# Attention scores from split operands: the low half of the keys multiplied on 64 partitions instead of 128, and the two PSUM banks of a row on opposite halves

## Chip, core and metric

The kernel runs on one core of one Trainium2 chip. What is measured is device time in microseconds of one execution of the whole program. A core has the engines TensorE (PE in the profile, its weight loads PEld), VectorE (DVE), ScalarE (ACT), GpSimd (POOL) and SyncE (SP), which work side by side and wait for each other through semaphores.

## What is computed

Two layers of a decoder trunk on 1024 tokens of width 1024. Of each layer, the attention part is what matters here:

```
z = rms_norm(x) @ w_in                       # q | k | v | u, 512 columns each
q, k normed and rotated per head             # 8 heads of 64
s = q @ k.T                                  # per head, 1024 x 1024, causal dilated masks
p = exp(s - max); att = (p @ v) / sum(p)
x = x + concat(att, pool) @ w_out
x = x + hier_moe(rms_norm(x))                # 16 experts, top 2 in one of 4 groups
```

The three dilated windows of the reference are one causal mask with logarithms of counts, which is added to the scores, so that each head needs one score matrix.

## The kernel before

Everything is written out by hand, engine by engine, in one loop over the two layers. A layer has four stages: the input projection (`in_pe`), attention (from `scores` to the last `probs_v`), the output projection with the router (`out_pe`), and the expert blocks (`moe_pe`).

**How scores are made.** TensorE takes operands of type fp32r, which hold fewer bits than fp32. So q and k are each split in a high part and a low rest, and a score is the sum of three products: high q with high k, low q with high k, high q with low k. A head has 64 channels and TensorE sums over up to 128 partitions. For head `a` of a pair (0 or 1), `own` are the 64 partitions where its q and k lie, `other` the 64 partitions of the other head. The tile `q_parts[a]` holds high q on `own` and low q on `other`; `k_high[a]` holds high k on `own` and a copy of k on `other`; `k_low[a]` holds low k on `own` and zeros on `other`. Two products then make one bank of scores: `q_parts` with `k_high` over 128 partitions gives two of the three terms (L1763), `q_parts` with `k_low` over 128 partitions gives the third (L1765), in which the 64 rows of `other` only add zeros. The zeros are written by two memsets on VectorE in each layer (L1165, L1262).

**Rows.** A row `m` (64 in a layer, `ROWS_A`) is one head's tile of 128 queries, number `i = m % 8`, against all keys up to its own: (i + 1) x 128, in steps of 256. So tiles 0 and 1 have one product pair of 256 columns, tiles 2 and 3 one of 512, tiles 4 and 5 one of 512 and one of 256 in a second PSUM bank, tiles 6 and 7 two of 512 in two banks. In a layer that makes 96 products of each of the two kinds, and 192 in the program.

**The order around them.** On TensorE the loop for row m has: `scores(m + 2)`, then `probs_t(m)` (turns of 128 x 128 of the probabilities, L1657), then `probs_v(m - 1)` (probabilities with v, 128 x 64, L1789), at some places `mix` (pooling, L1806) and `att_t`. VectorE adds the mask and takes the maximum (`mask`, L1278), evacuates half of the turned probabilities (L1288), and prepares the next head: `q_low` (L1254) and `k_lower` (L1243). ScalarE takes the exponential (`exp`, L899), evacuates the other half (L917), and prepares the next head: `q_top` (L838), `k_top` (L842) and `k_other` (L846), at places 8 to 10 and 0 to 2 of 16 rows. The semaphore `staged` tells TensorE that a head's low parts are there, `k_copied` that the copy of k is.

Of the kernel before, what the change touches and what calls it, by code (L numbers as in the profile page):

```python
# [33 lines left out]
P = 128  # L34
DEPTH, SEQ, D = 2, 1024, 1024
HEADS, HD = 8, 64
# [77 lines left out]
def trunk(nc, x, norm1_gain, w_in, q_norm_gain, k_norm_gain, w_pool, pool_scale, w_out,  # L114
# [7 lines left out]
    with ctx:  # L122
# [100 lines left out]
        k_low = [part("k_low0", AT_A + 5120, SEQ), part("k_low1", AT_H1 + 2 * SEQ, SEQ)]  # L223
        att = kT_r.rearrange("p (a t c) -> p a t c", a=PAIRS, c=P)
# [58 lines left out]
        k_copied = sem("k_copied")  # L283
        s_done = sem("s_done")
# [490 lines left out]
        def _(a_):  # L775
# [5 lines left out]
            for s in (params, k_copied, q_high_in, k_high_in, win_top, gain_in, sd1, sqz_done, sdz, cat_top, v_copied, u_copied, pool_top, t_evac, p_ready, pt0_ev, at_ev, sd2,  # L781
                      ge_exp, dm_exp, silu_done, aT_ready, y1_ready, xg_half, xg_top, gu_top, may_clear):
                a_.sem_inc(s, BIAS)
# [34 lines left out]
            with a_.Fori(0, DEPTH) as l:  # L818
# [28 lines left out]

                def in_act(t, par_, h):
# [43 lines left out]
                evac_turned(1, T - 1, 2)  # L892

# [15 lines left out]
                for m in range(ROWS_A):  # L909
# [17 lines left out]
                    if n == 2:  # L927
                        k_other(p, 1)
                    if p < PAIRS - 1:
                        if n == 10:  # L930
                            k_other(p + 1, 0)
                        if n == 8:
                            a_.wait_ge(s_done, upto(l, ROWS_A, p * 16 + 8))
                            q_top(p + 1, 0)
                        if n == 9:
                            k_top(p + 1, 0)
                    elif n == 10:
                        a_.wait_ge(poolT_ready, upto(l, 2 * NG, 2 * NG))
                        sc.activation(pool_hi, poolT[:, :, 0:P], ACT.Copy).then_inc(pool_top, 1)
# [165 lines left out]
        def _(dve):  # L1105
# [54 lines left out]
            def first_q_low(l):  # L1160
                dve.wait_ge(q_high_in, upto(l, 2 * PAIRS, 1))
                ve.tensor_tensor(out=q_parts[0][HD:P, :], in0=qT[0:HD, 0, :],
                                 in1=q_parts[0][0:HD, :].bitcast(f32), op=ALU.subtract)
                dve.wait_ge(z_done, upto(l, 4 * T, 4 * T - 2))
                ve.memset(k_low[0][HD:P, :].bitcast(f32), 0.0)  # L1165
# [66 lines left out]
            with dve.Fori(0, DEPTH) as l:  # L1232
# [6 lines left out]
                def k_lower(p, a, n, c=slice(0, SEQ)):  # L1239

                    own = slice(HD * a, HD * (a + 1))
                    dve.wait_ge(k_high_in, upto(l, 2 * PAIRS + 1, n))
                    return ve.tensor_tensor(out=k_low[a][own, c], in0=kT[own, p, c],  # L1243
                                            in1=k_high[a][own, c].bitcast(f32), op=ALU.subtract)
# [16 lines left out]
                dve.wait_ge(tqk_done, upto(l, 3 * T, 3 * T))  # L1261
                ve.memset(k_low[1][0:HD, :].bitcast(f32), 0.0)  # L1262
# [384 lines left out]
        def _(pe):  # L1647
# [29 lines left out]
            with pe.Fori(0, DEPTH) as l:  # L1677
# [74 lines left out]
                def scores(m):  # L1752
# [5 lines left out]
                    if m >= 2:  # L1758
                        pe.wait_ge(sm_ready, upto(l, ROWS_A, m - 1))
                    nk = (i + 1) * P  # L1760
                    for c in range(0, nk, 512):
                        w = min(512, -(-(nk - c) // 256) * 256)
                        te.matmul(ps[:, 2 * b + c // 512, 0:w], q_parts[a][:, i * P:(i + 1) * P],  # L1763
                                  k_high[a][:, c:c + w], start=True, stop=False)
                        ins = te.matmul(ps[:, 2 * b + c // 512, 0:w], q_parts[a][:, i * P:(i + 1) * P],  # L1765
                                        k_low[a][:, c:c + w], start=False, stop=True)
# [307 lines left out]
```

## Time and profile before

| | us |
|---|---|
| median of 3 runs | 1547.82 (1545.84 to 1548.75) |
| the profiled execution, its own time | 1546.53 |
| its span in the trace | 1544.7 |
| TensorE busy | 1408.9 (91%) |
| VectorE busy | 959.9 (62%) |
| ScalarE busy | 679.8 (44%) |
| GpSimd busy | 363.2 (24%) |

The span runs from the first to the last instruction. Busy is time in which an engine had an instruction of the program in work; TensorE's ends are modelled and overlap, so what a product costs is read from the distance between two starts. Within the span the attention stage of the first layer lies at 216 to 371 us and that of the second at 969 to 1123 us.

### The profile page before, as it was taken

Reading aid. Unit: us, or ns where it says so; the run is one execution under the profiler, and the core shown is the slowest. Engines: PE = TensorE matmul, PEld = TensorE weight load, DVE = VectorE, ACT = ScalarE, POOL = GpSimd, SP = SyncE. Lnnn points to the kernel's source line nnn. Section 1 sums busy time; section 2 is a strip of 40 time slices with the busy share of each in tenths; the row PEclk is TensorE's granted clock in tenths of the full one; section 3 lists DMA queues with packets and bytes.
Section 4 is the critical chain, followed back from the end, with each engine's and each line's share of the span. In section 5 each row is a group of like instructions: output and inputs, shape, how many; then the busy total and the mean of one; then the engine's idle time right before and its main releaser. Section 6 shows DMA issues by size and latency. Waiting matters only on the chain.

```text
span 1544.7 us, 23882 instructions
## 1 busy us (share of the span) xinstructions
PE 1408.9 (91%) x7375; PEld 1121.7 (73%) x7376; DVE 959.9 (62%) x1955; ACT 679.8 (44%) x1044; POOL 363.2 (24%) x256
## 2 busy tenths in 40 slices
PE   7999999999996899999699999899999959999990
PEld 5887878888885666666478788788888846666660
DVE  6666576663567756666566656766546686666560
ACT  5232156764112554555522312776621145554550
POOL 1000039302000133332520000870110013322335
PEclk9999999999998899999899999999999979999995
DMA  8200020000126999995581001200002577999827
GB/s 301 71 0 1 1 110 1 1 1 15 55 83 248 293 343 339 341 289 120 98 222 73 1 1 34 77 1 1 15 28 82 197 249 211 335 284 335 267 43 136
DMA packets 115892, 204.74 MB, mean 133 GB/s; under 512 B 9816, under 2 KB 76576, under 8 KB 115776
## 3 DMA queue, kind: packets, MB, share of 16 engines
q1 hardware_dynamic: 90976, 130.78, 24.4%
q0 software_dynamic: 19136, 53.67, 15.5%
q10 hardware_dynamic: 5664, 18.88, 3.1%
q8 instruction: 57, 0.93, 0.3%
q14 instruction: 59, 0.48, 0.1%
HBM read 169.74 MB, written 49.28 MB: 142 GB/s over the span
## 4 chain that ended last, share of the span: by engine, by line
PE 61%; DMA 16%; DVE 9%; issue 8%; ACT 4%; DVEq 1%; POOL 1%; ACTq 0%; POOLq 0%
PE ps L1687 19%; DMA out_x<-x_res,arena 15%; PE ps L1835 10%; PE ps L1657 9%; PE ps L1789 7%; PE ps L1965 6%; PE ps L1981 4%; PE ps L1763 2%; PE ps L1869 2%; PE ps L1765 2%; DVE w_in_lo L1157 1%; PE ps L1806 1%; ACT x_res L1004 1%; DVE arena L1375 1%; DVE gu_lo L1522 1%
## 5 line engine op out<-in xcount | busy, mean ns | idle before, releaser
L1522 DVE TENSOR_TENSOR gu_lo<-big,gu_hi 128x2048 fp32r<-128x2048 f32 x96 | 217.7, 2290 | 161.1 <-ACT gu_hi L982 149.9
L743 POOL DMA_INDIRECT x_res<-token_rows,row_tok x62 | 105.4, 1700 | 419.4 <-PE ps L1657 154.6
L982 ACT ACTIVATE gu_hi<-big 128x2048 fp32r (+1 forms) x96 | 180.7, 1916 | 29.0 <-PE ps L1965 17.9
L1657 PEld LDWEIGHTS ps<-cst,arena 128*128 128x128 f32 x970 | 112.4, 141 | 78.5 <-DVE arena L1587 27.4
L1657 PE MATMUL ps<-cst,arena 128*128 128x128 f32 x970 | 144.4, 275 | 26.1 <-DVE arena L1587 9.6
L1981 PE MATMUL ps<-big,arena 128*128 x360 | 163.8, 598 | 4.6 <-issue 4.6
L755 POOL DMA_INDIRECT out_x<-x_res,arena x62 | 101.6, 1639 | 188.6 <-ACT x_res L1004 137.6
L1278 DVE CUSTOM_DVE_ANT_0 arena<-ps,cst 128x128 f32<-128x128 f32 (+7 forms) x128 | 95.4, 754 | 79.2 <-PE ps L1765 78.5
L1789 PE MATMUL ps<-big,arena 128*128 128x64 f32 x1152 | 142.5, 269 | 0.0
L1789 PEld LDWEIGHTS ps<-big,arena 128*128 128x128 f32 x1152 | 138.5, 192 | 0.7
L1687 PE MATMUL ps<-w_in_hi,hT_hi 128*128 128x512 f32 x512 | 132.9, 399 | 3.9 <-ACT w_in_hi L803 2.5
L1687 PE MATMUL ps<-w_in_lo,hT_hi 128*128 128x512 f32 x512 | 129.5, 393 | 2.3 <-DVE w_in_lo L1157 2.2
L1687 PE MATMUL ps<-w_in_hi,hT_lo 128*128 128x512 f32 x512 | 126.7, 389 | 0.0
L1981 PEld LDWEIGHTS ps<-big,arena 128*128 128x128 f32 x360 | 65.5, 192 | 70.7 <-issue 70.7
L1687 PEld LDWEIGHTS ps<-w_in_lo,hT_hi 128*128 128x128 f32 x512 | 96.1, 189 | 25.3 <-DVE w_in_lo L1157 5.3
L1687 PEld LDWEIGHTS ps<-w_in_hi,hT_hi 128*128 128x128 f32 x512 | 94.6, 190 | 22.6 <-ACT w_in_hi L803 2.6
L1687 PEld LDWEIGHTS ps<-w_in_hi,hT_lo 128*128 128x128 f32 x512 | 96.1, 188 | 20.0
L899 ACT ACTIVATE arena<-arena,st 128x128 f32<-128x128 f32 (+7 forms) x128 | 98.8, 772 | 26.9 <-DVE st L1278 26.1
L1965 PE MATMUL ps<-gu_hi,xgT_hi 128*128 128x512 f32 x360 | 103.6, 410 | 7.6 <-issue 7.0
L1004 ACT ACTIVATE x_res<-ps 128x512 f32<-128x512 f32 x45 | 26.9, 598 | 182.2 <-DMA out_x<-x_res,arena 145.2
L1657 PE MATMUL ps<-cst,x_res 128*128 128x128 f32 x616 | 83.6, 280 | 19.3 <-DMA x_res<-token_rows,row_tok 11.5
L1965 PE MATMUL ps<-gu_lo,xgT_hi 128*128 128x512 f32 x360 | 98.5, 396 | 0.0
(199 smaller groups left out, 2350.7 us busy)
## 6 DMA issues: line engine op xcount, KB each, us to landing
big<-in_w_gate SPq DMA_DIRECT2D x32, 1024.0 KB, 11.4
big<-in_w_up SPq DMA_DIRECT2D x32, 1024.0 KB, 15.8
big<-in_w_down SPq DMA_DIRECT2D x32, 1024.0 KB, 13.8
big<-in_w_in SPq DMA_DIRECT2D x14, 1024.0 KB, 9.2
big<-in_w_out SPq DMA_DIRECT2D x4, 2048.0 KB, 10.3
token_rows<-arena ACTq DMA_DIRECT2D x16, 512.0 KB, 2.7
out_x<-x_res ACTq DMA_DIRECT2D x16, 512.0 KB, 3.5
x_res<-out_x SPq DMA_DIRECT2D x8, 512.0 KB, 5.3
```

Source lines behind the costliest of these rows:

```text
L743: pool.indirect_dma_start(out=xg[slot], out_offset=None, in_=token_rows, in_offset=bass.IndirectOffsetOnAxis(ap=row_tok[:, j:j + 1], axis= ...
L755: pool.indirect_dma_start(out=out, out_offset=bass.IndirectOffsetOnAxis(ap=row_dst[:, j:j + 1], axis=0), in_=y[j % RING], in_offset=None, ...
L899: sc.activation(pr[m % 3][:, 0:nk], pr[m % 3][:, 0:nk], ACT.Exp, scale=-1.0, bias=st[:, 64 + m % 16:65 + m % 16], accum_out=st[:, 80 + m % ...
L982: sc.activation(gu_hi[(2 * slot + h) % 3], raw, ACT.Copy).then_inc(gu_top, 1)
L1278: ve.tensor_tensor_reduce(out=pr[m % 3][:, 0:nk], in0=ps[:, 2 * b:2 * b + 2, :].rearrange("p a c -> p (a c)")[:, 0:nk], in1=cst[:, C_MASK ...
L1522: ve.tensor_tensor(out=gu_lo[i], in0=raw, in1=gu_hi[i].bitcast(f32), op=ALU.subtract)\
L1657: ins = te.transpose(ps[:, bank + i // 4, (i % 4) * P:(i % 4 + 1) * P], src, ident)
L1687: ins = te.matmul(ps[:, 2 + 2 * par_ + i, :], a[:, k, :], b[:, k, :], start=opens and k == 0, stop=closes and k == K - 1)
L1789: ins = te.matmul(ps[:, 6 + hd % 2, i * HD:(i + 1) * HD], prT[b][:, j, :], v[:, j, hd * HD:(hd + 1) * HD], start=j == 0, stop=j == i)
L1835: ins = te.matmul(ps[:, 2 * par_ + h, :], a, (hi, lo, hi)[n][:, k, :], start=opens and n == passes[0] and k == ks[0], stop=closes and n == ...
L1965: ins = te.matmul(ps[:, 2, :], a[:, h * K // 2 + k, :], b[:, k * 2 * FE:(k + 1) * 2 * FE], start=h == 0 and n == 0 and k == 0, stop=h == 1 ...
L1981: ins = te.matmul(ps[:, 4 + h, :], aT[:, k, :], big[:, ds(at + (E_GU + k * D + 512 * h), 512)], start=k == 0, stop=k == 1)
```

## The change

The low product runs over 64 partitions. For a row's first bank it takes high q and low k on `own`, as before, without the zeros. For the second bank it takes both operands on `other`: low k of keys 512 to 1023 is now written there (the columns 0 to 511 of `k_low` on `other`), and high q of queries 512 to 1023 is copied there by ScalarE (the columns 512 to 1023 of `k_low` on `other`, new function `q_other`, new semaphore `q_copied`). All high products of a row now come first, then all low ones. The two memsets go, `k_lower` writes its result in two instructions of 512 columns, and TensorE waits for `q_copied` before tile 4 of each head.

```diff
+                def q_other(p, a):
+                    own, other = heads(a)
+                    sc.activation(k_low[a][other, HALF:SEQ], qT[own, p, HALF:SEQ], ACT.Copy).then_inc(q_copied, 1)
...
+                q_other(0, 0)
...
+                    if n == 3:
+                        q_other(p, 1)
                     if p < PAIRS - 1:
                         if n == 10:
                             k_other(p + 1, 0)
+                        if n == 11:
+                            q_other(p + 1, 0)
...
-                dve.wait_ge(z_done, upto(l, 4 * T, 4 * T - 2))
-                ve.memset(k_low[0][HD:P, :].bitcast(f32), 0.0)
...
                 def k_lower(p, a, n, c=slice(0, SEQ)):
-                    own = slice(HD * a, HD * (a + 1))
+                    own, other = slice(HD * a, HD * (a + 1)), slice(HD * (1 - a), HD * (2 - a))
                     dve.wait_ge(k_high_in, upto(l, 2 * PAIRS + 1, n))
+                    if c.stop > HALF:
+                        ve.tensor_tensor(out=k_low[a][other, 0:HALF], in0=kT[own, p, HALF:SEQ],
+                                         in1=k_high[a][own, HALF:SEQ].bitcast(f32), op=ALU.subtract)
+                    c = slice(c.start, min(c.stop, HALF))
                     return ve.tensor_tensor(out=k_low[a][own, c], in0=kT[own, p, c],
                                             in1=k_high[a][own, c].bitcast(f32), op=ALU.subtract)
...
-                dve.wait_ge(tqk_done, upto(l, 3 * T, 3 * T))
-                ve.memset(k_low[1][0:HD, :].bitcast(f32), 0.0)
...
+                    if i == T // 2:
+                        pe.wait_ge(q_copied, upto(l, 2 * PAIRS, m // T + 1))
                     nk = (i + 1) * P
-                    for c in range(0, nk, 512):
-                        w = min(512, -(-(nk - c) // 256) * 256)
-                        te.matmul(ps[:, 2 * b + c // 512, 0:w], q_parts[a][:, i * P:(i + 1) * P],
-                                  k_high[a][:, c:c + w], start=True, stop=False)
-                        ins = te.matmul(ps[:, 2 * b + c // 512, 0:w], q_parts[a][:, i * P:(i + 1) * P],
-                                        k_low[a][:, c:c + w], start=False, stop=True)
+                    widths = [min(512, -(-(nk - c) // 256) * 256) for c in range(0, nk, 512)]
+                    for n, w in enumerate(widths):
+                        te.matmul(ps[:, 2 * b + n, 0:w], q_parts[a][:, i * P:(i + 1) * P],
+                                  k_high[a][:, 512 * n:512 * n + w], start=True, stop=False)
+                    own, other = slice(HD * a, HD * (a + 1)), slice(HD * (1 - a), HD * (2 - a))
+                    low_q = (q_parts[a][own, i * P:(i + 1) * P], k_low[a][other, i * P:(i + 1) * P])
+                    for n, w in enumerate(widths):
+                        ins = te.matmul(ps[:, 2 * b + n, 0:w], low_q[n], k_low[a][(own, other)[n], 0:w],
+                                        start=False, stop=True)
                     ins.then_inc(s_done, 1)
```

On TensorE, at tile 6 of the first head (the four score products of row 6, then the turns of row 4, then the first products with v), before:

```order
L1763 MATMUL ps<-k_high0_69,q_parts0_67 128x512
L1765 MATMUL ps<-k_low0_71,q_parts0_67 128x512
L1763 MATMUL ps<-k_high0_69,q_parts0_67 128x512
L1765 MATMUL ps<-k_low0_71,q_parts0_67 128x512
L1657 MATMUL ps<-cst,arena 128x128 x4
```

And the same place after the change:

```order
L1776 MATMUL ps<-k_high0_69,q_parts0_67 128x512 x2
L1781 MATMUL ps<-k_low0_71,q_parts0_67 128x512
L1781 MATMUL ps<-k_low0_71 128x512
L1668 MATMUL ps<-cst,arena 128x128 x4
```

The number of products is the same, and the high ones now stand together. The second low product reads both operands from `k_low`. The turns, which take all 128 partitions, follow directly on the low products in both.

On ScalarE, at places 3 and 4 of 16 rows (the exponential of row 4, 640 columns, the evacuation of row 3, and the exponential of row 5, 768 columns), before:

```order
L899 ACTIVATE arena,st<-arena,st 128x640
L917 ACTIVATE arena<-ps 128x512
L898 REGISTER_ALU
L899 ACTIVATE arena,st<-arena,st 128x768
L917 ACTIVATE arena<-ps 128x512
```

And after the change:

```order
L906 ACTIVATE arena,st<-arena,st 128x640
L924 ACTIVATE arena<-ps 128x512
L852 ACTIVATE k_low1_72<-big 64x512
L905 REGISTER_ALU
L906 ACTIVATE arena,st<-arena,st 128x768
L924 ACTIVATE arena<-ps 128x512
```

The new copy of 64 x 512 stands between the evacuation of row 3 and the exponential of row 5; there are eight such copies in a layer.

## Rows read from the trace of the kernel before

**Rows 1.** The page: busy time by engine, and the granted clock in 40 slices
```profile
PE 1408.9 (91%) x7375; PEld 1121.7 (73%) x7376; DVE 959.9 (62%) x1955; ACT 679.8 (44%) x1044; POOL 363.2 (24%) x256
...
PEclk9999999999998899999899999999999979999995
```

**Rows 2.** Busy time by stretch (us, PE, PEld, DVE, ACT, POOL, clock, DMA share): attention of both layers
```profile
216.00:372.00 156.00, 148.51 (x1100) 131.66 (x1101) 97.27 (x201) 107.66 (x222) 71.24 (x55) 1.00 0.04 15
964.00:1116.00 152.00, 143.63 (x1048) 126.28 (x1047) 97.50 (x204) 106.81 (x221) 63.05 (x46) 1.00 0.07 24
```

**Rows 3.** Timeline of TensorE, one tile of two full banks: start, length, line, form
```profile
304.27 0.48 PE L1763 MATMUL ps<-k_high,q_parts 128*128 128x512 f32 x1
304.59 0.40 PE L1765 MATMUL ps<-k_low,q_parts 128*128 128x512 f32 x1
304.82 0.40 PE L1763 MATMUL ps<-k_high,q_parts 128*128 128x512 f32 x1
305.06 0.39 PE L1765 MATMUL ps<-k_low,q_parts 128*128 128x512 f32 x1
305.29 0.27 PE L1657 MATMUL ps<-cst,arena 128*128 128x128 f32 x1
```

**Rows 4.** Timeline of the weight loads of the same tile
```profile
304.24 0.19 PEld L1763 LDWEIGHTS ps<-k_high,q_parts 128*128 128x128 f32 x1
304.36 0.19 PEld L1765 LDWEIGHTS ps<-k_low,q_parts 128*128 128x128 f32 x1
```

**Rows 5.** Timeline of TensorE, the second bank, of 256 columns, of a tile 5
```profile
222.17 0.28 PE L1763 MATMUL ps<-k_high,q_parts 128*128 128x256 f32 x1
222.28 0.28 PE L1765 MATMUL ps<-k_low,q_parts 128*128 128x256 f32 x1
```

**Rows 6.** Timeline at the program's start: turns over 128 partitions, then one over 40
```profile
8.28 0.63 PE L1657 MATMUL ps<-cst,x_res 128*128 128x128 f32 x2
...
8.49 0.42 PE L1657 MATMUL ps<-cst,x_res 128*128 128x128 f32 x1
...
8.84 0.18 PEld L1675 LDWEIGHTS ps<-cst,big 40*128 40x128 f32 x1 [0.33 <-issue]
```

**Rows 7.** Waits in 216 to 370 us: who for whom, us in total, times, longest
```profile
PEld ps L1657 <- ACT arena L899: 8.6, 12, 0.9
...
PEld ps L1763 <- DVE st L1278: 2.3, 4, 0.8
```

**Rows 8.** The chain of waits in 299 to 303.5 us: start, us, what
```profile
299.24 1.12 DVE q_parts L1254
...
300.47 0.35 DVE arena L1278
...
302.26 0.49 ACT arena L917
...
302.89 0.63 PE ps L1657 x4
```

**Rows 9.** Timeline of ScalarE and of VectorE at rows 3 to 5 of a head
```profile
320.13 1.06 ACT L846 ACTIVATE k_high<-big 64x1024 fp32r<-64x1024 f32 x1
...
322.64 0.58 ACT L917 ACTIVATE arena<-ps 128x512 f32<-128x512 f32 x1
323.82 0.94 ACT L899 ACTIVATE arena<-arena,st 128x768 f32<-128x768 f32 x1 [0.60 <-DVE st L1278]
...
321.69 1.22 DVE L1243 TENSOR_TENSOR k_low<-big,k_high 64x1024 fp32r<-64x1024 f32 x1
```

**Rows 10.** Timeline at the start of attention: VectorE and ScalarE
```profile
215.52 0.28 DVE L1243 TENSOR_TENSOR k_low<-big,k_high 64x128 fp32r<-64x128 f32 x1 [0.77 <-ACT k_high L842]
...
216.31 0.91 DVE L1262 MEMSET k_low<- 64x1024 f32 x1 [0.27 <-issue]
...
216.02 1.28 ACT L899 ACT_TABLE_LOAD   x1
217.41 0.40 ACT L899 ACTIVATE arena<-arena,st 128x128 f32<-128x128 f32 x1
```

More of the change, by code:

```diff
@@ L223, in trunk @@
         k_low = [part("k_low0", AT_A + 5120, SEQ), part("k_low1", AT_H1 + 2 * SEQ, SEQ)]
+        HALF = SEQ // 2
         att = kT_r.rearrange("p (a t c) -> p a t c", a=PAIRS, c=P)
@@ L283, in trunk @@
         k_copied = sem("k_copied")
+        q_copied = sem("q_copied")
         s_done = sem("s_done")
@@ L780, in _ @@
                     .then_inc(s_win[0][g], 16)
-            for s in (params, k_copied, q_high_in, k_high_in, win_top, gain_in, sd1, sqz_done, sdz, cat_top, v_copied, u_copied, pool_top, t_evac, p_ready, pt0_ev, at_ev, sd2,
+            for s in (params, k_copied, q_copied, q_high_in, k_high_in, win_top, gain_in, sd1, sqz_done, sdz, cat_top, v_copied, u_copied, pool_top, t_evac, p_ready, pt0_ev, at_ev, sd2,
                       ge_exp, dm_exp, silu_done, aT_ready, y1_ready, xg_half, xg_top, gu_top, may_clear):
```

## The prediction, made before the change was timed

> **What bounds the kernel now.** The page comes first. TensorE is busy 91% of the span, no other engine above 62%, and the granted clock is at its upper level of 2.4 GHz nearly throughout [rows 1]. The change touches attention alone, so the next view is busy time by stretch: TensorE 148.5 of 156.0 us in the first layer, 143.6 of 152.0 in the second, VectorE 97 and ScalarE 107 [rows 2]. So TensorE sets the pace of attention, with a few per cent of slack. Where the slack lies is told by the waits and by the chain of waits. In a layer TensorE's loads wait 8.6 us, in 12 places, for an exponential before the turns, and 2.3 us, in 4, for a mask before the next scores [rows 7]. The chain shows where: once per head, at rows 4 and 5, it leaves TensorE and runs through VectorE's low part of q, the mask of row 4, the exponential and ScalarE's evacuation, back to the turns [rows 8]. Everywhere else in attention it runs on TensorE. So a head has about 1.4 us of slack ((8.6 + 2.3) / 8), all around tiles 4 to 6, whose scores are made while VectorE and ScalarE are late. Tiles 0 to 3 and tile 7 are on the path, and time won or lost there counts in full.
>
> Last, what a product costs, by the distance of starts in the timeline. A product of 512 columns takes 0.23 us (304.59 to 304.82), the first of a tile 0.32 (304.27 to 304.59) [rows 3]. The 0.09 more is a weight load that isn't covered; the others are, since each load starts when the product before it starts, 0.12 after the load before [rows 4]. A product of 256 columns takes 0.11 [rows 5].
>
> **The change part by part.**
>
> Number of products: unchanged, 192 high and 192 low in the program. A product on 64 partitions streams as many columns as one on 128, so a low product alone gains nothing. The gain can come only from the two low products of a tile with two banks, if they run at the same time on the two halves of the array. Of the 128 tiles of both layers 64 have two banks. If the pair is perfect, tiles 6 and 7 save one product of 0.23, tiles 4 and 5 one of 0.11: per head 2 x 0.23 + 2 x 0.11 = 0.68, over 16 heads 10.9 us. Its second load is one more thing to cover: loads follow each other by 0.12 at best [rows 4], so if both loads begin only when the high products are done, the second product starts 0.12 after the first. Tiles 6 and 7 then save 0.11, tiles 4 and 5, whose second product is the short one, still 0.11.
>
> Switching between 128 and 64 partitions: this is new at every tile, once into the low products and once back to the turns, 256 times. Before, every product in the loop is on 128 partitions. The trace has one place where the height of the operand changes, at the program's start. There turns over 128 partitions follow each other by 0.21 us (8.28 to 8.49), and then a weight load of 40 partitions comes at 8.84, 0.35 after the last start, with 0.33 of idle time that no wait accounts for [rows 6]. By the step it should have been there by 8.70, and by the habit of rows 4 at 8.49. It looks as if the array ran empty before it took the new shape: 0.14 later than the end of streaming, and the load itself is no longer under the product before. The turns there follow each other more slowly than those in attention, of which four with the tail of the last take 0.63 [rows 8], so these are figures of a slower array, and I bound the emptying at full speed by half of it and by all of it, 0.07 to 0.14, and take 0.10. The uncovered load adds the 0.09 of rows 3. A switch is then 0.2 us (0.16 to 0.23). Below, the bound is zero, if the idle time of rows 6 has another reason; it is one row, and at the start of the program, when instructions may come late.
>
> The Trainium skill says in "TensorEngine Tiling (Array Packing)", section Tiling Modes, that a change of the tiling mode, other than one of the tile alone, drains the engine. It gives no duration; by it the switches would be paid and the sum would be that of the first case below, without it that of the third.
>
> The sum: tiles 0 to 3, 64 of them, gain nothing and pay two switches, 0.40 each: 25.6 us. Tiles 4 to 7, 64 of them, pay 0.40 and save 0.11: 0.29 each, 18.6 us. Together 44.2 us on TensorE. Against it stands the slack of tiles 4 to 6: three tiles of 0.29 are 0.87 per head, less than the mean slack of 1.4, but in some heads more than theirs; I take 0.8 per head as hidden, 16 heads, 12.8 us. That leaves 31.4 us.
>
> ScalarE: 16 copies of 64 x 512. One of 64 x 1024 takes 1.06 [rows 9], so about 0.6. The copy stands after the evacuation of row 3, which ends at 323.22, and ScalarE then waits 0.60 for the mask until 323.82 [rows 9]. It fits, and goes at nothing; without that cover it would delay row 5's exponential, at most 0.6 per head, 9.6 us. TensorE's new wait for it comes only at tile 4 of the next head, several rows later, and never ends last.
>
> VectorE: `k_lower` was 1.22 for 1024 columns [rows 9] and 0.28 for 128 [rows 10]; the line through both gives 0.15 fixed, so two halves cost 0.15 more. Eight times a layer, behind the mask of row 4 and before that of row 5, whose exponential isn't awaited by an idle TensorE: nothing on the path.
>
> Start of attention: the memset of 0.91 before the first mask goes [rows 10]. But ScalarE has the new copy of 0.6 before its table load of 1.28, which now ends at 217.30, just when the first exponential begins (217.41) [rows 10]. That exponential comes up to 0.6 later instead of earlier. Bound -0.9 to +0.6 a layer, taken as nothing. The other memset lies under input projection products.
>
> No DMA is added or moved; later stages begin later by what attention loses. The profiled execution took 1546.5, 1.3 below the median of the three runs, within their spread. Forecast: 1546.5 + 31.4 = 1578 us.
>
> **The rivals.** 0.2% of the time, 3.1 us, is about what a measurement of this kernel can tell from no change.
>
> 1. Every switch costs 0.16 to 0.23 and the pair overlaps in part (the forecast): 1578. With 0.16 the sum is 64 x 0.32 + 64 x 0.21 - 9 = 25 us, so 1571; with 0.23 and a pair that runs one after the other 128 x 0.46 - 14 = 45 us, so 1591. For it: rows 6, and that TensorE sets the pace. Against: a single row.
>
> 2. The switch is light: the array empties in part, but the load slips under the product before, say 0.07 each. Then 64 x 0.14 + 64 x 0.03 = 10.9, of which 1 to 3 are hidden: about 1555. The loads of rows 4, all covered, speak for it, the late load of rows 6 against.
>
> 3. Faster: switching costs nothing, and the second low product of a two-bank tile runs beside the first. Of the 10.9 us, what tiles 4 to 6 save (0.45 per head) falls into slack, since the turns wait for VectorE and ScalarE there [rows 8]; only tile 7's 0.23 is sure, 16 x 0.23 = 3.7, and perhaps 1 to 2 more from the memset and from heads with little slack: 1541, at best 1536. It decides for this side where a switch costs less than about 0.03 us (128 tiles with two each against 3.7 to 10.9 us). The Trainium skill, in the same page's Theoretical Speedup, gives up to 2 times for operands of 64 rows; by it the pair is perfect and this case holds if switching is free. No product here runs on half the array, so no row tests it.
>
> 4. The change doesn't do what it says: products on two halves run one after the other, and switching is free. Then only small terms are left, 1546 to 1548.
>
> **How the numbers follow.** Case 1: 0.57. Case 2: 0.15. Case 3: 0.20, of which 0.16 beyond 3.1 us. Case 4: 0.08. Faster 0.16, same 0.12 (case 4 and the rest of case 3), slower 0.72. The likeliest case's own range is 1564 to 1594: its two bounds, wider by the copy's 9.6 us if uncovered in part, and by more slack than I took. The whole range reaches down through case 2 and case 4 to the middle of case 3: 1541 to 1595; outside lie half of case 3 and the most costly end of case 1, under 0.2.
>
> **What would show each step right or wrong.** If case 1 holds, the weight load of the first low product starts 0.3 us or more after the start of the last 512-wide high product, where before it started with it; the same at the first turn after the low products, except at rows 4 and 5, where it waits anyhow. Attention is longer by some 16 us in each layer, the other stages as before. TensorE's waits for ScalarE and VectorE in rows 7 shrink to a third. The two low products of a two-bank tile start about 0.12 apart, where a pair that doesn't overlap would show 0.23. ScalarE's idle 0.60 before row 5's exponential is gone, and nobody waits for the copy. The prediction is wrong if the load of the first low product starts with the high product before it: then there is no emptying, and the time falls to case 3 or 4. If switches come to over 0.3 each, the time is above the range.

## The result, and the profile after

| | before | after |
|---|---|---|
| median of 6 runs | 1548.72 us (1545.84 to 1553.82) | 1624.05 us (1598.11 to 1655.27) |
| mean granted clock of the span | 0.971 (profiled) | 0.909 to 0.949 |
| profiled execution, its own time | 1546.53 us | 1655.27 us |

The ratio is 1.039 with a 95% interval of 1.036 to 1.042; it leaves out the three longest runs of the changed kernel. Slower was forecast, but 1624 lies above the range of 1541 to 1595: the kernel became 75 us longer, where 31 were forecast. What is new beside the mean is the spread: 57 us between the shortest and the longest run, 8 before.

The page of the kernel after, busy time and granted clock in 40 slices:

```profile
PE 1529.0 (92%) x7375; PEld 1187.1 (72%) x7376; DVE 962.3 (58%) x1967; ACT 694.9 (42%) x1060; POOL 351.3 (21%) x256
...
PEclk9999965699999799999899998557999989999995
```

Against [rows 1] TensorE has 120 us more busy time for the same 7375 products, and the clock has two new dents, slices 6 to 8 and 25 to 28. Busy time by stretch (us, PE, PEld, DVE, ACT, POOL, granted clock, DMA share, GB/s) shows that the dents are the beginnings of the two attention stages:

```profile
216.00:320.00 104.00, 102.93 (x401) 82.50 (x400) 40.03 (x80) 47.54 (x96) 60.23 (x45) 0.52 0.05 18
320.00:424.00 104.00, 103.74 (x712) 81.37 (x711) 59.34 (x129) 68.55 (x138) 9.73 (x11) 1.00 0.02 6
1020.00:1136.00 116.00, 115.19 (x434) 90.24 (x434) 44.93 (x89) 51.68 (x104) 60.71 (x45) 0.51 0.05 16
1136.00:1232.00 96.00, 95.85 (x667) 75.86 (x665) 54.22 (x120) 63.94 (x128) 8.08 (x10) 1.00 0.02 7
```

For about 100 us of each layer TensorE ran at its lower level of 1.2 GHz, with hardly any idle time by the profile (102.93 of 104.00 us busy, though a product's end is modelled, so that short pauses between products don't show): 401 products in 104 us, then 712 in the next 104. From the first to the last product with v attention took 201.1 us in the first layer and 206.3 in the second, where it took 151.9 and 152.0 before. That is 103.5 of the profiled 108.8 us.

The timeline at full clock shows the switches. First TensorE's products at a tile with two full banks, then its weight loads, then the products at a tile with one bank of 256:

```profile
350.93 0.71 PE L1776 MATMUL ps<-k_high,q_parts 128*128 128x512 f32 x2
351.57 0.50 PE L1781 MATMUL ps<-k_low,q_parts 64*128 64x512 f32 x1
351.57 0.49 PE L1781 MATMUL ps<-k_low 64*128 64x512 f32 x1
352.06 0.30 PE L1668 MATMUL ps<-cst,arena 128*128 128x128 f32 x1
```
```profile
351.57 0.18 PEld L1781 LDWEIGHTS ps<-k_low,q_parts 64*128 64x128 f32 x1 [0.37 <-issue]
351.57 0.18 PEld L1781 LDWEIGHTS ps<-k_low 64*128 64x128 f32 x1
352.03 0.20 PEld L1668 LDWEIGHTS ps<-cst,arena 128*128 128x128 f32 x2 [0.28 <-issue]
```
```profile
353.78 0.36 PE L1776 MATMUL ps<-k_high,q_parts 128*128 128x256 f32 x1
354.07 0.38 PE L1781 MATMUL ps<-k_low,q_parts 64*128 64x256 f32 x1
354.39 0.33 PE L1668 MATMUL ps<-cst,arena 128*128 128x128 f32 x1
```

Three things are to be seen. The low load doesn't start with the last high product, as loads did in [rows 4], but 0.37 of idle time after the load before it. The two half-height loads start together, and so do the two products: the pair overlaps perfectly, load and product. And after the pair the turns' load again comes late, 0.46 after it. From the first high product to the first turn a tile with two full banks takes 1.13 us, where [rows 3] has 1.02; a tile of one 256 takes 0.61, and 0.32 before (327.45 to 327.77 us in that trace). So a pair almost pays for its switches, and a lone half-height product doesn't at all.

The same products at half clock:

```profile
248.01 0.77 PE L1776 MATMUL ps<-k_high,q_parts 128*128 128x512 f32 x1
248.71 0.79 PE L1781 MATMUL ps<-k_low,q_parts 64*128 64x512 f32 x1
```

0.70 from the high to the low one.

Per head (from the first product with v to that of the next head, read from starts in the trace):

| head | 0 | 1 | 2 | 3 | 4 | 5 | 6 |
|---|---|---|---|---|---|---|---|
| before, layer 1 | 18.9 | 18.3 | 21.0 | 19.5 | 20.5 | 19.1 | 19.6 |
| after, layer 1 | 34.2 | 34.2 | 34.2 | 20.4 | 21.5 | 20.5 | 20.6 |
| after, layer 2 | 34.2 | 34.2 | 37.5 | 22.3 | 21.5 | 20.4 | 20.6 |

At full clock (heads 3 to 7 of layer 1, the last of which takes 15.3 us instead of 14.7) the change costs 1.0 us a head. A head wholly at half clock takes 34.2 instead of 20.5, so that each microsecond at half clock costs (34.2 - 20.5) / 34.2 = 0.40 us.

ScalarE's new copy lies where it was expected:

```profile
390.73 0.58 ACT L924 ACTIVATE arena<-ps 128x512 f32<-128x512 f32 x1
391.33 0.63 ACT L852 ACTIVATE k_low<-big 64x512 fp32r<-64x512 f32 x1
392.32 0.94 ACT L906 ACTIVATE arena<-arena,st 128x768 f32<-128x768 f32 x1 [0.36 <-DVE st L1289]
```

0.63 for it, and ScalarE still waits for VectorE behind it.

### The profile page after: what moved, and what is told of

It reads as the page before. It is cut to its first block, busy times and chain, and to the rows that moved or that the text cites. A ratio compares the mean times of both kernels' runs of the same rounds, so it can differ in the third digit from the quotient of the medians.

```text
span 1653.5 us, 23925 instructions
## 1 busy us (share of the span) xinstructions
PE 1529.0 (92%) x7375; PEld 1187.1 (72%) x7376; DVE 962.3 (58%) x1967; ACT 694.9 (42%) x1060; POOL 351.3 (21%) x256
## 4 chain that ended last, share of the span: by engine, by line
PE 70%; DMA 12%; DVE 7%; issue 5%; ACT 2%; DVEq 1%; POOL 1%; ACTq 0%; POOLq 0%
PE ps L1698 18%; PE ps L1668 12%; DMA out_x<-x_res,arena 10%; PE ps L1805 10%; PE ps L1851 9%; PE ps L1981 8%; PE ps L1997 5%; PE ps L1781 3%; PE ps L1776 3%; PE ps L1885 1%; DVE w_in_lo L1168 1%; PE ps L1822 1%; DVE arena L1386 1%; DVE gu_lo L1533 1%; DMA big<-in_w_in 1%
## 5 line engine op out<-in xcount | busy, mean ns | idle before, releaser
L1668 PE MATMUL ps<-cst,arena 128*128 128x128 f32 x970 | 174.7, 314 | 18.3 <-DVE arena L1598 12.0
L1668 PEld LDWEIGHTS ps<-cst,arena 128*128 128x128 f32 x970 | 125.6, 158 | 89.7 <-issue 48.0
L745 POOL DMA_INDIRECT x_res<-token_rows,row_tok x62 | 99.1, 1599 | 420.7 <-PE ps L1668 156.7
L1805 PE MATMUL ps<-big,arena 128*128 128x64 f32 x1152 | 184.6, 320 | 0.0
L1805 PEld LDWEIGHTS ps<-big,arena 128*128 128x128 f32 x1152 | 183.7, 244 | 0.0
L924 ACT ACTIVATE arena<-ps 128x512 f32<-128x512 f32 (+3 forms) x128 | 65.7, 513 | 153.8 <-PE ps L1668 153.1
L1997 PEld LDWEIGHTS ps<-big,arena 128*128 128x128 f32 x360 | 66.1, 194 | 71.6 <-issue 71.6
L1668 PE MATMUL ps<-cst,x_res 128*128 128x128 f32 x616 | 83.2, 279 | 19.9 <-DMA x_res<-token_rows,row_tok 11.6
## 6 DMA issues: line engine op xcount, KB each, us to landing
big<-in_w_out SPq DMA_DIRECT2D x4, 2048.0 KB, 10.2
```

The source lines that it names most:

```text
L745: pool.indirect_dma_start(out=xg[slot], out_offset=None, in_=token_rows, in_offset=bass.IndirectOffsetOnAxis(ap=row_tok[:, j:j + 1], axis= ...
L1668: ins = te.transpose(ps[:, bank + i // 4, (i % 4) * P:(i % 4 + 1) * P], src, ident)
L1805: ins = te.matmul(ps[:, 6 + hd % 2, i * HD:(i + 1) * HD], prT[b][:, j, :], v[:, j, hd * HD:(hd + 1) * HD], start=j == 0, stop=j == i)
L1997: ins = te.matmul(ps[:, 4 + h, :], aT[:, k, :], big[:, ds(at + (E_GU + k * D + 512 * h), 512)], start=k == 0, stop=k == 1)
```

## The experiments

The theories after the result: the switches let the clock fall by the idle time of the array at each emptying (A), or the products of half height do so (B); and beside the clock some full-clock part is larger than forecast (C). Medians are of 4 timed runs, where nothing else is said, beside the kernel before on the same chip (medians of 7 runs, 1547 to 1550 us; one of those 7, beside four of the experiments, took 3152 us, which nothing here explains). The expectations below say "pair" or "head pair" where one head is meant, as in the table above. In the fences of two stretches the columns are those of the stretches above, the first line is layer 1's attention, the second layer 2's.

**Full height everywhere.**

```diff
-                        ins = te.matmul(ps[:, 2 * b + n, 0:w], low_q[n], k_low[a][(own, other)[n], 0:w],
+                        ins = te.matmul(ps[:, 2 * b + n, 0:w], q_parts[a][:, i * P:(i + 1) * P], k_low[a][:, 0:w],
```

> The changed kernel with every low product over 128 partitions (q_parts with the first 512 columns of k_low), its order, copies, waits and VectorE halves kept; the second bank's low part is thus made from other keys than it should be. It takes away the change of array shape alone. If switching and the clock that falls with it are the whole loss: 1545 to 1552 us, granted clock in attention 1.0, the load of a low product starting with the product before it. If the ScalarE copy, the reordering or the memsets matter: attention over 3 us longer than before with all products on full height, 1555 or more.

Measured: 1564.66 us, ratio 1.012 (1.008 to 1.016), clock 0.962 to 0.970.

```profile
219.00:378.00 159.00, 148.88 (x1091) 131.18 (x1090) 100.15 (x200) 109.70 (x223) 67.55 (x49) 0.99 0.02 7
978.00:1136.00 158.00, 148.82 (x1089) 131.75 (x1088) 99.72 (x199) 108.93 (x222) 66.56 (x49) 0.98 0.02 6
```

The clock stays up but for three short falls of 3.4 us, so the change of shape is what keeps it down for long. But the time isn't back: 15 us are left without any change of shape. Heads 0 to 2 take 19.9, 22.7 and 21.9 us, the later ones what they took before. The groups of VectorE's low part of k, first in this kernel in 216 to 284 us (three heads, two pieces each), then in the kernel before in 216 to 284 (four heads) and in 284 to 370:

```profile
L1253 DVE TENSOR_TENSOR k_low<-big,k_high 64x512 fp32r<-64x512 f32 x3 | 6.5, 2157 | 0.1
L1256 DVE TENSOR_TENSOR k_low<-big,k_high 64x512 fp32r<-64x512 f32 x3 | 5.6, 1861 | 0.0
```
```profile
L1243 DVE TENSOR_TENSOR k_low<-big,k_high 64x1024 fp32r<-64x1024 f32 x4 | 8.7, 2178 | 0.1
...
L1243 DVE TENSOR_TENSOR k_low<-big,k_high 64x1024 fp32r<-64x1024 f32 x3 | 3.7, 1220 | 0.1
```

While GpSimd works (pooling and the split of w_out, the first 60 us or so of attention), one piece of half the size takes 1.9 to 2.2 us on average, as much as the whole did (1.4 to 3.3, 2.2 on average), and the two together 4.0. Later, two take 0.69 each. The Trainium skill states in "SBUF — State Buffer", section "SBUF: two separate sides", that VectorE with two inputs from SBUF and a GpSimd instruction that reads SBUF lock each other out for the length of an instruction. The durations agree with it; where inside an instruction the waiting falls they don't show.

At its worst, in head 1, the two pieces hold up the mask and with it TensorE (two rows of VectorE, one of TensorE):

```profile
243.64 2.78 DVE L1253 TENSOR_TENSOR k_low<-big,k_high 64x512 fp32r<-64x512 f32 x1
246.43 2.28 DVE L1256 TENSOR_TENSOR k_low<-big,k_high 64x512 fp32r<-64x512 f32 x1
249.64 1.01 PE L1776 MATMUL ps<-k_high,q_parts 128*128 128x512 f32 x2 [2.88 <-DVE st L1289]
```

At 249.9 us, right behind this pause, the clock falls for 3.4 us.

**Low k in one piece again.** The kernel above, with `k_lower` over 1024 columns and the memsets at half their width.

```diff
-                    if c.stop > HALF:
-                        ve.tensor_tensor(out=k_low[a][other, 0:HALF], in0=kT[own, p, HALF:SEQ],
-                                         in1=k_high[a][own, HALF:SEQ].bitcast(f32), op=ALU.subtract)
-                    c = slice(c.start, min(c.stop, HALF))
...
+                ve.memset(k_low[0][HD:P, 0:HALF].bitcast(f32), 0.0)
```

> The kernel with every low product over 128 partitions, but low k made in one VectorE instruction of 1024 columns again and the memsets back at half their width; ScalarE's copy of q and the order of products stay as in the change. The run with full height came 15 us above the kernel before; its trace shows low k taking 4.5 and 5.1 us in two pieces while GpSimd works, against 3.3 and 1.5 in one. If the two pieces are that loss: 1546 to 1552 us, the second and third head pair stretch back to 18.3 and 21.0 us. If the copy on ScalarE or the order is it: it stays at 1560 or more.

Measured: 1548.25 us, ratio 0.999 (0.996 to 1.002); heads 0 to 2 take 18.9, 17.8 and 21.0 us.

```profile
219.00:371.00 152.00, 145.87 (x1091) 129.75 (x1091) 93.47 (x192) 109.65 (x224) 67.83 (x49) 1.00 0.02 8
973.00:1124.00 151.00, 145.69 (x1087) 129.98 (x1085) 93.21 (x192) 108.85 (x222) 66.82 (x48) 0.99 0.02 6
```

So the two pieces cost 16 us, and ScalarE's copy, the order of products and the start of attention cost nothing together. That is a first part of (C). Some 5 of the 16 us are clock: by the mean granted clocks full height in two pieces has 104 us at half clock, in one piece 91, at 0.40 each.

**Half height without a partner.** No copy of q, low k whole on `own`, both banks' low products there.

```diff
-                        ins = te.matmul(ps[:, 2 * b + n, 0:w], low_q[n], k_low[a][(own, other)[n], 0:w],
+                        ins = te.matmul(ps[:, 2 * b + n, 0:w], q_parts[a][own, i * P:(i + 1) * P],
+                                        k_low[a][own, 512 * n:512 * n + w],
```

> Low products over the 64 own partitions for both banks, one after the other, no copy of q, no second half of k_low: the zeros are dropped and nothing else. Theory that half-height products let the clock fall: it falls as in the changed kernel, and more columns run at half height with no partner, so attention is as long or longer (1610 to 1660 us). Theory that the emptying lets it fall: two switches per tile as in the changed kernel, the gaps the same, the fall the same or a little less, since the array is longer busy between gaps. At full clock the two low products of a two-bank tile start 0.23 apart instead of together, 0.23 (512) or 0.11 (256) more per tile.

Measured: 1656.54 us (1641.61 to 1705.59), clock 0.888 to 0.925, the lowest of all kernels here, though its low k is in one piece.

```profile
220.00:434.00 214.00, 213.85 (x1088) 168.86 (x1087) 93.22 (x192) 106.96 (x215) 65.13 (x49) 0.73 0.01 5
1034.00:1222.00 188.00, 185.48 (x1089) 146.93 (x1088) 95.10 (x194) 106.99 (x215) 67.70 (x49) 0.86 0.02 6
```

A head at full clock (head 5) takes 21.1 us against 20.4 with pairs: 0.63 more, and an unshared pair should cost 2 x 0.23 + 2 x 0.11 = 0.68. The overlap of the pair is thus real, and it is all that the change wins. One figure of the expectation is missed: in a tile of two full banks the two low products start 0.34 apart (383.96 and 384.30 us), not 0.23, as the second product of a run of one shape does in [rows 3] (0.32); the turns then follow after 0.32 instead of 0.43 to 0.49 behind a pair, and the two nearly cancel. Of the two theories the time fits the first, for the fall is longer than in the changed kernel and not a little less; but run by run the times at half clock overlap (246 to 382 us here, 163 to 301 there).

**Emptying without a change of shape.** The kernel before, all products at full height, high ones first, with TensorE waiting for its own products before the low ones and again before the turns.

```diff
+                    ins.then_inc(high_done, 1)
+                    pe.wait_ge(high_done, upto(l, ROWS_A, m + 1))
...
                 def probs_t(m):
+                    pe.wait_ge(s_done, upto(l, ROWS_A, min(m + 3, ROWS_A)))
```

> The kernel before, all products over 128 partitions, high products first, then a wait of TensorE for its own high products, then the low ones, and before the turns a wait for its own scores: the array runs empty twice per tile without any change of shape. If gaps of TensorE are what lets the clock fall: it falls to 0.5 in attention as in the changed kernel, the time is 1600 us or more. If it is the half height: the clock stays at 1.0 in attention, and the time rises only by the gaps, 128 tiles x 2 x 0.2 to 0.3 us less slack, 1580 to 1600 us.

Measured: 1634.06 us (1606.42 to 1647.22), clock 0.941 to 0.966. The steps at full clock (a tile of one 256), and the two stages:

```profile
331.42 0.36 PE L1764 MATMUL ps<-k_high,q_parts 128*128 128x256 f32 x1
331.84 0.39 PE L1769 MATMUL ps<-k_low,q_parts 128*128 128x256 f32 x1
332.29 1.09 PE L1658 MATMUL ps<-cst,arena 128*128 128x128 f32 x8
```
```profile
221.00:404.00 183.00, 175.81 (x1083) 131.82 (x1083) 92.77 (x192) 107.11 (x214) 67.64 (x48) 0.96 0.01 4
1009.00:1194.00 185.00, 177.62 (x1082) 133.13 (x1083) 95.23 (x192) 106.67 (x214) 67.42 (x48) 0.95 0.01 4
```

The waits make longer gaps than the switches do (0.42 and 0.45 between starts, against 0.29 and 0.32 in the changed kernel), and a head at full clock takes 23.2 us. Both theories got something right: the clock does fall at the start of attention, for 17 and 21 us in the profiled run, which (B) did not expect; but it comes back in head 0 of both layers and then stays at 1.0 through heads with some 4 us of gaps each, which (A) did not expect. Nor is the time mostly clock: heads 3 to 7 are 3.5 us longer than before by the gaps alone, 56 us over 16 heads, which leaves about 29 of the 85.

**One wait per tile.** The first of the two waits alone.

```diff
+                    ins.then_inc(high_done, 1)
+                    pe.wait_ge(high_done, upto(l, ROWS_A, m + 1))
```

> The kernel before with high products first and one wait of TensorE for its own high products before the low ones: one emptying per tile, all products over 128 partitions. With two waits the time was 1606 to 1647 us and a mean granted clock of 0.941 to 0.966. If emptying alone brings the clock down in proportion, the mean clock is between that and the 0.971 of the kernel before, and the time 1570 to 1600 us. If full-height products hold the clock against one gap a tile: clock 0.968 to 0.972, time 1565 to 1575 us, by the gaps alone (128 x 0.2 less slack).

Measured: 1577.88 us, ratio 1.019 (1.017 to 1.021), clock 0.959 to 0.973 (5 runs).

```profile
220.00:396.00 176.00, 171.51 (x1089) 141.69 (x1088) 95.09 (x193) 106.60 (x215) 67.25 (x49) 0.92 0.01 5
999.00:1166.00 167.00, 162.32 (x1086) 132.27 (x1085) 94.55 (x192) 106.20 (x215) 67.68 (x48) 0.97 0.02 5
```

The time and four of the five clocks (one is 0.973, the others 0.959 to 0.967) lie where the first expectation has them, but the clock is the smaller part: heads 3 to 7 are 1.5 us longer by the gaps, 25 of the 31 us. The profiled run, the longest of its five, has 27 us at half clock in one piece. Emptying once per tile is enough to bring the clock down now and then.

**Half the switches: pairs alone, and lone products alone.** In the first, tiles 0 to 3 make their low product over 128 partitions; in the second, tiles 4 to 7 do.

```diff
+                        if len(widths) == 1:
+                            ins = te.matmul(ps[:, 2 * b, 0:w], q_parts[a][:, i * P:(i + 1) * P], k_low[a][:, 0:w],
+                                            start=False, stop=True)
+                            continue
```

> The changed kernel with the low products of tiles 0 to 3 over 128 partitions (they add products of two low parts, which are of no size), pairs on two halves kept for tiles 4 to 7: half the switches, and every half-height product has a partner. If lone half-height products let the clock fall: the clock stays at 1.0, and the time is 1546 plus 64 tiles x about 0.1 to 0.2 us less slack, 1550 to 1556 us. If it is the gaps: half of them are left, and the clock falls for a shorter time or in some runs, 1555 to 1600 us.

> Half height in tiles 0 to 3 alone, where a half-height product has no partner; tiles 4 to 7 make their low products over 128 partitions (their second bank from other keys). As many switches as with pairs alone (two in 64 tiles), so equal emptying. If half height without a partner is what holds the clock down: clearly more time at 0.5 in attention than with pairs alone (which had 14 and 31 us in its two layers), 60 us or more in the two layers together, 1590 us or more. If only the emptying counts: the same time at 0.5, 1565 to 1585 us.

Measured: pairs alone 1572.79 us, ratio 1.016 (1.011 to 1.021), clock 0.956 to 0.966; lone products alone 1580.76 us, ratio 1.020 (1.017 to 1.023), clock 0.958 to 0.962. In the profile of pairs alone the clock is down for 3.4 and 10.2 us in layer 1 and for 17.1 and 13.7 in layer 2, in that of lone products alone for 6.8 and 23.9 and for 3.4 and 3.4. Pairs alone, then lone products alone:

```profile
220.00:380.00 160.00, 151.99 (x1084) 126.25 (x1082) 99.35 (x199) 109.36 (x222) 65.95 (x48) 0.97 0.01 5
983.00:1148.00 165.00, 160.59 (x1083) 133.63 (x1083) 96.88 (x199) 110.24 (x222) 67.12 (x48) 0.91 0.02 6
```
```profile
220.00:393.00 173.00, 167.16 (x1089) 142.07 (x1089) 98.50 (x199) 109.77 (x222) 66.94 (x49) 0.92 0.02 5
993.00:1156.00 163.00, 157.23 (x1088) 132.88 (x1089) 97.15 (x199) 109.59 (x222) 66.47 (x49) 0.98 0.02 6
```

The clock doesn't tell them apart: 0.97 and 0.91 against 0.92 and 0.98. That a lone half-height product is worse for the clock than a pair is not borne out. What halving the switches does is plain, though: in the profiled runs the clock is down in attention for 44 and 38 us instead of 212. And head 5, at full clock, gives the prices: 19.3 us with pairs alone, 20.4 with lone products alone, 19.1 before. Of the 1.0 to 1.3 us a head that the switches cost, tiles 0 to 3 cost nearly all.

**More work on purpose.** The first kernel adds a partner to each lone product of heads 0, 1, 2 and 7, the second makes the high product of tiles 0 to 3 twice.

```diff
+                    if len(widths) == 1 and m // T in (0, 1, 2, 7):
+                        ins = te.matmul(ps[:, 2 * b + 1, 0:w], q_parts[a][other, i * P:(i + 1) * P],
+                                        k_low[a][other, 0:w], start=True, stop=True)
```
```diff
+                        if len(widths) == 1:
+                            te.matmul(ps[:, 2 * b + n, 0:w], q_parts[a][:, i * P:(i + 1) * P],
+                                      k_high[a][:, 512 * n:512 * n + w], start=True, stop=True)
```

> The changed kernel plus a partner product on the other half of the array for each half-height product of tiles 0 to 3 in heads 0, 1, 2 and 7 (low q with low k into the second bank, which nobody reads): 64 products more, the switches and the emptying unchanged. If the clock answers to how much of the array works: little or no fall in the first three heads, 1565 to 1590 us, faster than the changed kernel (1598 to 1655) though it does more. If it answers to the emptying alone: the fall stays, 1600 us or more. If the partners don't run at the same time, each costs 0.1 to 0.23 us, at most 11 us.

> The changed kernel with the high product of tiles 0 to 3 made twice, full height, the second over the first: 64 products more, on the path, 32 x 0.23 + 32 x 0.11 = 11 us at full clock, switches unchanged. If the clock answers to how much of the array works over time: less time at 0.5, 1575 to 1610 us, no slower or faster than the changed kernel in spite of the 11 us. If it answers to the emptying alone: 1620 to 1670 us.

Measured: with partners 1617.07 us (1605.76 to 1622.20), clock 0.933 to 0.949; with high products twice 1612.45 us (1599.99 to 1622.78), clock 0.941 to 0.957. With partners, then with high products twice:

```profile
220.00:394.00 174.00, 170.85 (x1102) 135.20 (x1101) 97.37 (x199) 110.49 (x222) 67.23 (x49) 0.91 0.02 5
994.00:1177.00 183.00, 178.28 (x1097) 141.93 (x1097) 99.08 (x199) 110.35 (x222) 66.22 (x48) 0.87 0.01 5
```
```profile
222.00:427.00 205.00, 205.00 (x1113) 163.09 (x1113) 98.38 (x199) 110.55 (x221) 63.90 (x47) 0.76 0.01 4
1026.00:1195.00 169.00, 163.31 (x1112) 128.29 (x1112) 98.81 (x199) 110.10 (x222) 66.82 (x48) 0.99 0.01 5
```

Neither brings the clock back. Both kernels do more and aren't slower than the changed one, by medians 7 and 12 us faster, but all their times lie within its spread. Partners cost nothing at full clock: the last head takes 15.3 us with and without them. By their own expectations the kernel with partners (1600 us or more) speaks for the emptying alone, and the one with high products twice (1575 to 1610, or 1620 to 1670) falls between. This is inconclusive as to (B).

**The changed kernel again**, for a second profile.

> The changed kernel once more, for a second profile: the first had 99 and 113 us at half clock in its two attention stages and 1655 us. The heads that run wholly at either clock should take the same time as before (34.2 us a pair at half, 20.4 to 20.6 at full from the seventh head on); how long the clock is down should differ, and the time with it by 0.4 us for each us.

Measured: 1622.59 us (2 runs, 1614.20 and 1630.99), clock 0.943 and 0.926.

```profile
221.00:395.00 174.00, 169.85 (x1087) 134.48 (x1087) 98.27 (x199) 109.56 (x221) 67.26 (x49) 0.92 0.01 4
998.00:1188.00 190.00, 187.20 (x1087) 148.80 (x1087) 98.65 (x199) 111.15 (x222) 67.00 (x49) 0.82 0.02 5
```

As expected: heads 3 to 6 take 20.4 to 21.5 us as in the first profile, and only the time at half clock differs, 31 and 68 us instead of 99 and 113. The spread of the changed kernel is how long the clock stays down.

**What the runs give together.** Time at half clock is 2 x (1 - mean clock) x span. Means over the timed runs: 91 us for low k in one piece (the same as before: nearly all its dents lie outside attention), 104 for full height, 107 with one wait, 123 for pairs alone, 126 for lone products alone, 157 with two waits, 168 with high products twice, 195 with partners, 228 for the changed kernel, 296 for half height without a partner. That the emptying lets the clock fall is shown by the waits at full height. That half height adds to it is likely: the changed kernel has shorter gaps than the kernel with two waits and a lower clock (0.909 to 0.949 in 8 runs against 0.941 to 0.966 in 4). Half height without a partner is the cleaner comparison, since it too has low k in one piece: 0.888 to 0.925. It isn't shown apart from emptying, since no kernel here has half height without switches.

Where the clock falls is the same in all twelve profiles. A fall in attention begins in a pause of TensorE of 0.8 to 2.9 us, or within 4 us of its end, and there are only two such places: the start of attention, with a pause of 0.78 us, and head 1, where TensorE waits for a mask behind VectorE's low part of k, beside a busy GpSimd. Here is the second one with pairs alone; the clock falls at 247.9 us:

```profile
245.90 1.00 PE L1809 MATMUL ps<-big,arena 128*128 128x64 f32 x8
249.78 1.22 PE L1776 MATMUL ps<-k_high,q_parts 128*128 128x512 f32 x2 [2.88 <-DVE st L1289]
```

None begins later than 37 us after the first product with v, although the switches or waits go on through all eight heads. The kernel before has the pause of 0.78 us too, and no fall there; at full height without waits a fall lasts 3.4 us, with switches or waits 3.4 to 116. So the switches don't bring the clock down by themselves. They make a fall at a pause likelier and above all longer. What else these two places have in common no run varies, and whether a changed kernel without the pauses would keep its clock is open.

The 75 us thus divide into 16 for two pieces of low k, 16 for the switches at full clock (1.0 a head, 16 heads), and the rest, some 43, for the clock. Worked from the clock itself it is (228 - 91) x 0.40 = 55. The two ways differ because 5 of the 16 us for the pieces are clock as well, and because the pieces seem to cost nothing in a head at half clock: it takes 34.2 us with two pieces, and without a partner, in one piece, 35.5, which is 1.3 more, just twice the 0.63 of full clock. By the three shortest runs alone (some 60 us longer, 188 us at half clock) the clock's part is (188 - 91) x 0.40 = 39. These are estimates.

No kernel here is faster than the one before. Low k in one piece at full height is the same within 0.3%.

## Why the prediction was wrong, by its own steps

**What bounds the kernel**: right. Attention alone moved, and TensorE sets its pace. But "the granted clock is at its upper level nearly throughout" was read as a property of the kernel, and carried over to the changed one without a word. This is the step that failed: no case, and no bound, held a fall of the clock, which was worth 39 to 55 us, although the same rows show that it falls elsewhere (dents in [rows 1]), and although the forecast itself put idle time into the array 256 times.

**Switches**: right in kind. The load of the first low product was to come 0.3 us or more after the last high product's start, and the emptying was put at 0.10. Measured is 0.33 (351.24 to 351.57), with the high product streaming for 0.23 of it: 0.10. The one row at the program's start was good evidence. The size of the sum was off, 31.4 for 16. From its first product to that of the next tile, each tile with one bank takes 0.34 to 0.35 longer (head 6 of layer 1, by the starts in the trace), where 0.40 was forecast: 0.17 a switch. The pair's loads start together instead of 0.12 apart, and a head without the overlap costs 0.63 more, where 0.44 was counted as saved. Tiles 4 to 7 come out even: +0.20, +0.01, -0.39 and +0.16, the -0.39 at tile 6, where TensorE waited before (the turns came 0.72 after the last low product, 322.64 to 323.36 us) and now hardly does (0.49). That makes 0.9 to 1.4 a head, where 31.4 us is 2.0. "If switches come to over 0.3 each, the time is above the range" was the only sign given for such a time, and they don't.

**VectorE: "nothing on the path"**: wrong, 16 us. The duration of 1.22 came from a head at 321 us, after GpSimd had finished. The same instruction takes longer in the same trace where GpSimd works:

```profile
221.89 3.28 DVE L1243 TENSOR_TENSOR k_low<-big,k_high 64x1024 fp32r<-64x1024 f32 x1
```

and 2.48 at 260.07 us. A split instruction was priced by its columns, though in that stretch each instruction, however short, seems to wait anew.

**ScalarE, start of attention, DMA**: right, nothing. Only the sign for it was off: the idle 0.60 before row 5's exponential is not gone but 0.2 to 0.4.

That the errors in the switches and in VectorE's part cancel (16 + 16 for 31.4) is chance. Without the clock the time would have been about 1575 to 1580, an estimate from the parts above.

**The rivals**: the faster one had the pair right, and the time wrong, for switching isn't free. Case 2 put a switch at 0.07, and it costs 0.17. Case 4 falls with the pair that starts together.

## What to carry to other kernels

Before a change puts small gaps or half-height products into a stretch that is bound by TensorE, ask what it does to the granted clock: here 16 us of gaps brought some 40 to 55 us more, and a spread of 57 us. Look for the pauses of a microsecond or more that such a stretch already has, for there the clock fell. Two products on opposite halves do run at the same time, loads included, but a switch of height costs about 0.17 us, of which 0.1 is emptying, so such products should stand in long runs of one shape (which no run here tries). And a duration is taken from the stretch where the instruction will stand: what VectorE does beside a busy GpSimd goes more by the instruction than by the column.

## What the runs showed of the hardware that was not expected

- Weight loads for the two halves start together: 351.57 and 351.57 us, where loads at full height are 0.12 apart.
- The lower clock can hold for 100 us under a TensorE that the profile shows busy for 102.93 of 104.00 us, with two switches in every tile, in a program that is at full clock in the next 104 us with the same instructions. It came back 4 us before head 3 in the first layer and 4 us into it in the second.
- With waits at full height the clock fell for 17 and 21 us and then held at 1.0 with over 0.4 us between starts at every wait. Between runs of the changed kernel the time at half clock varied from 163 to 301 us, of which some 91 lie outside attention.
- All falls of the clock in attention began at two pauses of TensorE, of 0.78 us at its start and of 0.9 to 2.9 us in head 1, and none in the heads behind.
